# A decoder layer on one core: 42 instead of 32 tokens in the second gathered tile

## The reference

```
def peer(a, w_q, k1, k2, u_exp, v_exp):
    ... # per token and head: the 16 best of 128 x 128 product keys -> experts, gates (softmax of the 16 scores)
        u_sel = jnp.take(u_exp, e_c, axis=0)
        h = jnp.einsum('bthkd,btd->bthk', u_sel, a_c, ...)
        w = (g_c * jax.nn.gelu(h)).astype(a_c.dtype)
        v_sel = jnp.take(v_exp, e_c, axis=0)
        return jnp.einsum('bthk,bthkd->btd', w, v_sel)
    ...
h = h + peer(rmsnorm(h, g_ffn), w_peer_q, k1, k2, peer_u, peer_v)
```

## Time and profile before

| | |
|---|---|
| median of 3 runs | 3002.78 us (2994.18 to 3005.68) |
| the profiled execution | 2995.07 us, its span 2992.9 us |
| mean granted TensorE clock | 0.998 of full speed |
| PE, DVE, ACT, POOL busy | 99%, 74%, 42%, 48% |
| memory traffic | 798 MB, 745 MB of it read |
| u slots with picks and adds of gates | 1061 to 1652 us |
| the last u slots | to 1780 us |
| v slots with picks | 1780 to 2704 us |
| the rest (v, projection, gate, norm) | to 2993 us |

### The profile page before, as it was taken

The page is one execution under the profiler, slowest core; times in us unless marked ns, Lnnn a source line. Parts: engine busy times, 40 slices in busy tenths (PEclk is TensorE's granted clock), DMA queues, the critical chain, the costliest instruction groups (busy, mean ns, idle before and its releaser), DMA issues. The chain is left out here.

```text
span 2992.9 us, 43288 instructions
## 1 busy us (share of the span) xinstructions
PE 2950.2 (99%) x16888; PEld 2771.6 (93%) x16888; DVE 2220.2 (74%) x2801; ACT 1255.1 (42%) x1818; POOL 1435.3 (48%) x813
## 2 busy tenths in 40 slices
PE   9999999999999999999999999999999999999998
PEld 7888668889999999999999999999999999999787
DVE  5465664578878777777777669888888888986445
ACT  5224542333333333333333334555555555554422
POOL 1010000008888888888888125665555667660000
PEclk9999999999999999999999999999999999999999
DMA  8462222235445599999999889999999999994222
GB/s 297 169 241 86 71 85 98 99 123 125 128 125 137 132 338 339 361 354 364 358 349 362 329 306 412 406 410 403 407 410 408 402 407 401 400 381 152 97 96 99
DMA packets 205172, 798.01 MB, mean 267 GB/s; under 512 B 68208, under 2 KB 121472, under 8 KB 128736
## 3 DMA queue, kind: packets, MB, share of 16 engines
q1 hardware_dynamic: 90768, 405.36, 36.2%
q0 software_dynamic: 95440, 367.63, 34.0%
q10 hardware_dynamic: 18816, 23.11, 2.2%
HBM read 745.46 MB, written 50.51 MB: 266 GB/s over the span
## 5 line engine op out<-in xcount | busy, mean ns | idle before, releaser
L1745 PE MATMUL ps<-aH,wH 128*128 128x352 f32 (+2 forms) x3088 | 1062.0, 344 | 6.9 <-DVE wL L1048 6.9
L1747 PE MATMUL ps<-aH,wL 128*128 128x352 f32 (+2 forms) x3088 | 1059.1, 343 | 0.0
L1746 PE MATMUL ps<-aL,wH 128*128 128x352 f32 (+2 forms) x3088 | 1059.0, 343 | 0.0
L1048 DVE TENSOR_TENSOR wL<-raw,wH 128x2048 fp32r<-128x2048 f32 x333 | 787.5, 2365 | 224.6 <-ACT wH L626 221.9
L540 POOL DMA_INDIRECT gates<-gates_r,idx_d x384 | 753.9, 1963 | 377.9 <-DVE gates_r L1463 243.0
L626 ACT ACTIVATE wH<-raw 128x2048 fp32r<-128x2048 f32 x333 | 636.8, 1912 | 677.2 <-PE ps L1747 581.2
L1745 PE MATMUL ps<-actH,wH 128*128 128x352 f32 x2048 | 662.2, 323 | 3.2 <-DVE wL L1048 3.2
L1747 PE MATMUL ps<-actH,wL 128*128 128x352 f32 x2048 | 661.9, 323 | 0.0
L1746 PE MATMUL ps<-actL,wH 128*128 128x352 f32 x2048 | 661.4, 323 | 0.0
L1745 PEld LDWEIGHTS ps<-aH,wH 128*128 128x128 f32 x3088 | 581.2, 188 | 47.8 <-DVE wL L1048 6.6
L1747 PEld LDWEIGHTS ps<-aH,wL 128*128 128x128 f32 x3088 | 580.9, 188 | 38.1
(11 more groups left out here) (273 smaller groups left out, 2433.2 us busy)
## 6 DMA issues: line engine op xcount, KB each, us to landing
raw<-s_pu SPq DMA_DIRECT2D x128, 1024.0 KB
raw<-s_pv SPq DMA_DIRECT2D x128, 1024.0 KB
gates<-zeros POOLq DMA_DIRECT2D x22, 1024.0 KB, 8.6
pre<-ut ACTq DMA_DIRECT2D x128, 176.0 KB
pre_in<-pre SPq DMA_DIRECT2D x128, 176.0 KB
gate_in<-gates SPq DMA_DIRECT2D x128, 176.0 KB
raw<-s_out SPq DMA_DIRECT2D x16, 1024.0 KB
raw<-s_pq SPq DMA_DIRECT2D x16, 1024.0 KB
```

What stands on the lines that cost most here:

```text
L1048: V.tensor_tensor(wL[parity][:, :], src[:, :], wH[parity][:, :].bitcast(F), ALU.subtract).then_inc(lo_ready, 1)
L1745: mm(out, wh, xh, start=start, stop=False, skip_group_check=skip_group_check)
L1746: mm(out, wh, xl, start=False, stop=False, skip_group_check=skip_group_check)
L1747: return mm(out, wl, xh, start=False, stop=stop, skip_group_check=skip_group_check)
```

## The change

The second gathered tile holds 42 tokens instead of 32. 128 partitions hold 3 sets of 42, with 2 partitions over; 3 sets share 128 picks as 43, 43 and 42. So there are 128 + 43 = 171 picks in place of 160, and 342 dense columns in place of 352. Everything else follows: the index and gate arrays of the second tile are cleared first, since the third set leaves one pick empty; the two unused partitions of `b_rep` are set to zero; `sel` is built later, at the first pick of the second tile; 16 x 42 sums no longer fit one bank and use two.

```
-BT = 32
+BT = 42
-B_PICKS = A_PICKS // SETS
+B_PICKS = -(-A_PICKS // SETS)
+SPAN = SETS * BT
...
 @block.gpsimd
+            nc.gpsimd.memset(idx_b[:, :], 0).then_inc(b_cleared, 1)
+            nc.gpsimd.memset(gates_b[:, :], 0.0).then_inc(b_cleared, 1)
...
 def bring_set(i):
-                src = slice(i * B_PICKS, (i + 1) * B_PICKS)
-                act.dma_start(idx_b[dst, :], idx_e[at_b:P, src]).then_inc(b_loaded, 16)
-                act.dma_start(gates_b[dst, :], gates_r[at_b:P, NTD - 1, src]).then_inc(b_loaded, 16)
+                src = slice(i * B_PICKS, min((i + 1) * B_PICKS, A_PICKS))
+                n = src.stop - src.start
+                if i == 0:
+                    act.wait_ge(b_cleared, 2)
+                act.dma_start(idx_b[dst, 0:n], idx_e[at_b:P, src]).then_inc(b_loaded, 16)
+                act.dma_start(gates_b[dst, 0:n], gates_r[at_b:P, NTD - 1, src]).then_inc(b_loaded, 16)
...
 def spread_tokens():
-                r4 = b_rep[:, :, :].rearrange("p k (r t) -> p k r t", t=BT)
+                r4 = b_rep[:, :, 0:SPAN].rearrange("p k (r t) -> p k r t", t=BT)
+                if SPAN < P:
+                    st.did(V.tensor_scalar(b_rep[:, :, SPAN:P], hT[:, :, TD:TD + P - SPAN], 0.0, None, ALU.mult))
...
-                V.tensor_reduce(sel[:, :], ident[:, :].rearrange("p (r t) -> p t r", t=BT), AX, ALU.add).then_inc(sel_ready, 1)
...
 def dot(j):
                 if j == A_PICKS:
+                    dve.wait_ge(b_loaded, 32 * SETS)
+                    V.tensor_reduce(sel[:, :], ident[:, 0:SPAN].rearrange("p (r t) -> p t r", t=BT), AX, ALU.add).then_inc(sel_ready, 1)
...
 (v group 15, slot 2)
-                        V.tensor_tensor(hT[:, :, TD:TA], hT[:, :, TD:TA],
-                                        ps[:, BACK[0], 0:KD * BT].rearrange("p (k t) -> p k t", t=BT), ALU.add).then_inc(b_added, 1)
+                        for r in range(2):
+                            ks = slice(8 * r, 8 * r + 8)
+                            V.tensor_tensor(hT[:, ks, TD:TA], hT[:, ks, TD:TA],
+                                            ps[:, BACK[r], 0:8 * BT].rearrange("p (k t) -> p k t", t=BT), ALU.add).then_inc(b_added, 1)
```

More of the change, by code:

```diff
@@ L253, in trunk_layer @@
     idx_b = at("idx_b", [B_PICKS], U32, C0 + 12 * KB + 576)
[L254 to L257, removed]
+    gates_b = at("gates_b", [B_PICKS], F, C0 + 12 * KB + 768)
+    dots_b = at("dots_b", [B_PICKS], F, C0 + 14 * KB + 1472)
+    pick_wb = at("pick_wb", [B_PICKS], F, C0 + 14 * KB + 1664)
+    sel = at("sel", [BT], F, C0 + 14 * KB + 864)
     identR = at("identR", [P], R, C0 + 13 * KB)
@@ L325, in trunk_layer @@
         dot_done, dot_gelu, pick_weighed, pick_done = sem("dot_done"), sem("dot_gelu"), sem("pick_weighed"), sem("pick_done")
-        b_loaded, rep_ready, b_tok_done, b_tok_early, b_tok_ready = (
-            sem("b_loaded"), sem("rep_ready"), sem("b_tok_done"), sem("b_tok_early"), sem("b_tok_ready"))
+        b_cleared, b_loaded, rep_ready, b_tok_done, b_tok_early, b_tok_ready = (
+            sem("b_cleared"), sem("b_loaded"), sem("rep_ready"), sem("b_tok_done"), sem("b_tok_early"), sem("b_tok_ready"))
         sel_ready, b_sum_done, b_added = sem("sel_ready"), sem("b_sum_done"), sem("b_added")
@@ L985, in _ @@
                 if q == 2:
-                    act.wait_ge(b_added, 1)
+                    act.wait_ge(b_added, 2)
                 for k in ((), (), (0, 1, 2, 3, 4))[q] if q < 3 else (2 * q - 1, 2 * q):
@@ L1479, in spread_tokens @@
                                        .to_broadcast([P, KD, SETS, BT]), ALU.mult))
-                V.tensor_reduce(sel[:, :], ident[:, :].rearrange("p (r t) -> p t r", t=BT), AX, ALU.add).then_inc(sel_ready, 1)
                 st.settle()
-                r3 = b_rep[:, :, :].rearrange("p k (r t) -> p (k r) t", t=BT)
-                V.tensor_tensor(r3, r3, rstd[:, TD:TA].unsqueeze(1).to_broadcast([P, KD * SETS, BT]), ALU.mult).then_inc(rep_ready, 1)
+                V.tensor_tensor(r4, r4, rstd[:, TD:TA].unsqueeze(1).unsqueeze(2).to_broadcast([P, KD, SETS, BT]), ALU.mult).then_inc(rep_ready, 1)
             HS = 2 + HEAD_U
@@ L1648, in _ @@
                         dve.wait_ge(b_sum_done, 1)
-                        V.tensor_tensor(hT[:, :, TD:TA], hT[:, :, TD:TA],
-                                        ps[:, BACK[0], 0:KD * BT].rearrange("p (k t) -> p k t", t=BT), ALU.add).then_inc(b_added, 1)
-                        dve.wait_ge(b_added, 1)
+                        for r in range(2):
+                            ks = slice(8 * r, 8 * r + 8)
+                            V.tensor_tensor(hT[:, ks, TD:TA], hT[:, ks, TD:TA],
+                                            ps[:, BACK[r], 0:8 * BT].rearrange("p (k t) -> p k t", t=BT), ALU.add).then_inc(b_added, 1)
+                        dve.wait_ge(b_added, 2)
                     for k in range(0 if q == 2 else 2 * q - 2, 2 * q):
@@ L2093, in _ @@
                 if q == 1:
-                    pe.wait_ge(back_copied, 1)
+                    pe.wait_ge(back_copied, 2)
                     pe.wait_ge(sel_ready, 1)
                     for k in range(KD):
-                        ins = mm(ps[:, BACK[0], k * BT:(k + 1) * BT], b_acc[:, k, :], sel[:, :], start=True, stop=True)
+                        ins = mm(ps[:, BACK[k // 8], k % 8 * BT:(k % 8 + 1) * BT], b_acc[:, k, :], sel[:, :], start=True, stop=True)
                     ins.then_inc(b_sum_done, 1)
```

## The result

The changed kernel takes 3150.66 us (median of 4 runs, 3135.76 to 3157.63), the kernel before 2998.48 us beside it (4 runs, 2994.16 to 3005.68): a ratio of 1.0498, 95% interval 1.0453 to 1.0544. The forecast was 3034 with a range up to 3066. The direction was right, the size was not: 152 us more instead of 32.

A forecast was written before the change was run, and what follows sets the result against it. PE sets the pace now, with DMA full; the v slots with picks become DMA bound. Terms -7 - 3.4 + 44 - 2 + 0.4 = +32 us on 3002.78 give 3034; range 2968 to 3066.

The forecast's parts named there:

- The heads and the u slots to 1652 us: Stretch up to the end of POOL's gate adds: 7 us gained, bounds 6 and 22.
- The 1.4 us for an earlier first head: Before the gate adds: first head routed 1.4 us earlier, after some 7 narrower slots.
- a width of 342 for the matmul: Rival: a 342-column matmul costs as one of 352; gains vanish, +44, 3047; counted within the main forecast's range.
- POOL hardly stops: U slots: POOL runs on from its first add to 1652 us, with 0.3 us of issue between instructions.
- The last u slots: 1652 to 1780 us, after POOL's adds: 17 slots x 0.20 = 3.4 us gained.
- The v slots: With 11 more picks, DMA bound at 955 us: +44, bounds -21 and +56; last ten slots, gathers over: 2 us gained.
- 20 KB a slot and 2.4 MB in all: V slots: bytes saved by chunks of `pre` and `gates` losing ten columns; credited 3 us.
- The rival of a little room in DMA: V slots: 419 GB/s can be held, so +14.5 there, +2.5 in all, 3005; chance 0.20.
- DVE only waits more often: V slots: DVE needs 7.13 us of a slot of 8.03 us, so it doesn't stop the stage.
- queued behind a late row: V slots: next `wL` waits on DVE behind a late gathered row and PE waits for it; no size given.
- DVE waiting for `u_rows`: Sign that the forecast was right, in the v slots with picks; no size given.
- The signs: If right: matmuls 0.1558 us apart, v-slot DMA some 406 GB/s, PE below 94%, adds over at about 1645 us.

The follow-up runs named there:

- experiment 1: Changed kernel with gate rows padded to 352, so third-tile adds have 96 indices again: 3043.67 us, ratio 1.0129; P (first matmul of the v slots) at 1791.1 us.
- experiment 2: Kernel before with only the third tile's gate adds cut from 96 to 86 indices: 3108.13 us, ratio 1.0345; first v matmul at 1891.9 us.
- The width ruler: Kernel before with v-slot matmuls from 352 down to 326 columns by group; only spacing read: 160.0 ns at 352, 157.8 at 342.
- experiment 13: Kernel before with only the matmuls of u slots 32 to 127 narrowed to 342 columns: 3000.73 us, ratio 0.9990.
- experiments 8 and 9: Changed kernel, gate rows padded: v-slot DVE accumulation halved, 3034.11 us; that plus half the gathered v-row bytes and both DRAM arrays padded, 2973.57 us.
- experiment 6: Changed kernel with gate rows padded to 352 and the last 11 gathered picks left out (160 picks): 2992.66 us, ratio 0.9957.
- experiment 8: Changed kernel with gate rows padded to 352 and DVE's accumulation of v rows in the v slots halved, all bytes kept: 3034.11 us, ratio 1.0112.
- experiment 7: Changed kernel with gate rows padded to 352 and v-slot gathers bringing half of each v row, read twice: 3042.64 us, ratio 1.0133.

## Why the forecast was wrong

**The step that failed** is the add in "The heads and the u slots to 1652 us". It said "3.4 ns an index, so 128 x 10 x 3.4 ns = 4.4 us" gained, from two points, 128 and 96. Both are multiples of 16, so they could not show what another count does. Measured: +1.02 us for each of the 128 adds (2.45 less 1.43 at the shortest), +116 us in the group. The 1.4 us for an earlier first head did not show either: the first add starts at 677.10 us, before at 674.14. The bounds "6, and 22" were both gains. They had no end for an instruction that the trace of before does not have; a width of 342 for the matmul was given such an end, a count of 86 for the add was not.

**What carried it to the end** was read rightly: "POOL hardly stops", "arrives late", "there is no lead left". For that reason next to nothing of the 116 us was hidden: experiment 1 gives 106 us of P for it and experiment 2 112. The sign of the term was wrong, its path was right.

**The last u slots** were to give 3.4 us, and the u slots as a whole 10.4, of which the adds 4.4. With the adds put right P is 1 to 16 us later than before instead. Some 10 us of that can be scatter; the gain, at any rate, is not seen. The width ruler takes part of it away (2.2 ns a matmul instead of 4.17), the full DMA perhaps another (experiment 13). How much each has is not settled.

**The v slots** were forecast at +44 while gathers run and -2 for the last ten; they came to +42.5 (951.7 us from the first matmul to the last gather, 909.2 before) and -4.5, together +38. The stretch with gathers before and after, columns as in the earlier trace rows:

```profile
1779.80:2689.00 909.20, 906.01 (x5650) 904.43 (x5649) 786.66 (x534) 502.80 (x866) 551.48 (x309) 1.00 1.00 403
```

```profile
1897.30:2849.00 951.70, 912.46 (x5677) 895.20 (x5676) 841.20 (x570) 504.06 (x891) 589.42 (x332) 1.00 1.01 409
```

The mechanism was right: with DVE relieved the stage stays at 1025 us until bytes are taken off too (experiments 8 and 9), and experiment 6 gives 45 us for the 11 picks. That the size is so near is in part luck, for two small errors go opposite ways. The chunks do not lose "20 KB a slot and 2.4 MB in all": ten columns of 128 partitions are 5 KB and two arrays 10 KB a slot, 1.2 MB in all; over the whole run q1 moved 404.05 MB instead of 405.36. That makes 389 MB, and 958 us at the assumed 406 GB/s instead of 955. But the rate over the 951.7 us was 409, and 414 in the middle. The rival of a little room in DMA, +14.5 at 419 GB/s, is thereby true to a small part; whether the rate rose because more was asked for, or because gathers now have 57.3% of DMA's time from 2000 to 2500 us instead of 54.4%, is not shown.

**DVE.** "DVE only waits more often" is nearly what experiment 8 shows: halving its accumulation gives 7.6 us. It becomes a bound only in experiment 7, with fewer bytes and with POOL's products beside its own. The road by which DMA reaches PE was read wrongly, though: "queued behind a late row". The waits from 1900 to 2833 us of the changed kernel:

```profile
POOL pre_in L588 <- DMA gate_in<-gates: 266.6, 86, 9.5
ACT actH L885 <- POOL pre_in L588: 158.1, 64, 6.0
...
DVE actL L1588 <- ACT actH L885: 97.9, 69, 6.4
...
PE ps L1755 <- DVE wL L1054: 37.2, 48, 4.0
...
DVE rows L1560 <- DMA rows<-u_rows,idx_b: 5.1, 8, 1.5
DVE rows L1560 <- DMA rows<-u_rows,idx_s: 4.2, 8, 0.8
```

"DVE waiting for `u_rows`" was named as a sign, and these are 9 us in all: the lateness comes by `gate_in`, POOL's product and ACT, not by rows. DVE's waits for `actH` were 63.8 us in the v slots with picks before.

**The signs**: matmuls 0.1578 us apart instead of 0.1558; 414 GB/s instead of some 406; the adds over at 1772 instead of 1645, which no sign had foreseen on that side; PE at 96% instead of below 94%.

## What to carry to other kernels

A size that becomes the number of partitions or indices of a transfer is a number with divisors, not a length: before choosing it, look for the largest divisor up to 16, and pad the array rather than cut the count. Two points of one kind in a trace don't price a third of another kind; give it a bound on the dear side. When a stage has two bounds near each other, relieving either shows little, and only both together tell; and an experiment that relieves one engine may slow another, so compare the lengths of its instructions before taking the result for a bound.

## What the hardware showed that was not expected

- An indirect add of single numbers costs POOL 1.43 us at 96 indices, 2.46 at 86, 4.71 at 127 and 1.59 at 126: about 27 ns for each unit of count / largest divisor up to 16, with 16 packets for each unit.
- DMA brought 415 GB/s at a share of 1.02, where in the kernel before, with fewer gathers in the mix, it had been at 406 with 1.01: a full share did not mean the highest rate.
- Matmuls of 342 and of 344 columns both stood 157.8 ns apart, those of 340 columns 155.0.
- A DVE `tensor_tensor` of 128x342 took 0.51 us, and 1.38 us on average when POOL's product of the same shape ran beside it.
- While PE had next to nothing to do, from 1061 to 1110 us, its granted clock was 0.69 on average.
